# Hybrid Mamba-2 and attention trunk on eight cores: second half's z projection brought forward, one conv tap moved off VectorE, halo taps batched, a new instruction order

## The chip, the cores and the metric

The kernel runs on the 8 cores of one Trainium2 chip. Each core takes one of the 8 sequences of the batch whole, so the cores run the same program on different data and exchange nothing. The time is the device time of the slowest core in microseconds (us). The median of the runs of one kernel is what is compared.

## What is computed

The trunk has two layers over 2048 tokens of width 1024. What matters here is the first layer's mixer and the two feed-forward blocks:

```python
def mamba2_mixer(h, in_proj, conv_w, conv_b, dt_bias, A_log, D, gnorm, out_proj):
    zxbcdt = h @ in_proj
    z, xBC, dt = jnp.split(zxbcdt, [SSM_INNER, SSM_INNER + SSM_CONV_DIM], axis=-1)
    xBC = jax.nn.silu(causal_dwconv(xBC, conv_w, conv_b))          # width 4
    ...
    y = ssd_chunked(xs, dt, A, Bm, Cm) + xs * D[:, None]           # scan over chunks
    y = group_rms_norm(y * jax.nn.silu(z), gnorm, SSM_GROUPS)      # 8 groups
    return y @ out_proj

def conv_ffn(x, norm_g, w_in, conv_w, conv_b, w_down):
    gate, val = jnp.split(rms_norm(x, norm_g) @ w_in, [FFN_DIM], axis=-1)
    gate = causal_dwconv(gate, conv_w, conv_b)                     # width 3
    return (jax.nn.silu(gate) * val) @ w_down
```

x gains mixer(norm(x)), then conv_ffn; the second layer gains a sliding-window attention with rotary positions and a second conv_ffn. z of a token needs only the normed input of that token; the conv of a token needs the three tokens before it; the scan carries a state from chunk to chunk.

## The kernel before

**Work and stages.** The 2048 tokens are cut into two halves of 1024. The mixer's 8 channel groups g times 2 halves h give 16 units, in the order of `units` (all groups of half 0, then all of half 1). The program is laid out in five stages, marked at the end of `build`: A0 (units 0 to 7, with the projection of unit 8), A1+F00 (units 8 to 15 beside the output projection and the feed-forward of half 0), F01+T0 (output projection and feed-forward of half 1 beside the attention of half 0), F10+T1 (second feed-forward of half 0 beside the attention of half 1), F11 (second feed-forward of half 1, alone).

**A unit** has two parts. `P_gen(i)` projects: four conv kinds (two of x, then B, then C), each 16 matmuls of 128x512 into a pair of PSUM banks; ScalarE takes the pair out with bias and the last tap's weight into `acc` (L264), VectorE adds the other three taps from PSUM with a `scalar_tensor_tensor` each (`stt`, L279), ScalarE applies SiLU. Then z: 64 matmuls of 128x256 in two tiles, and SiLU into `zB`. The last three columns of a half 0 conv go to `halo_m`; in half 1 each of the three taps adds its halo with a small `stt` of 3, 2 or 1 columns. `S_gen(i)` does the scan: `S_head` transposes x and B by DMA on SP's queue (`xk`, `Bt`, L325) and scales on GpSimd (`xdd`), `S_exp` builds the decays for the next unit (`E`), `S_core` runs the chunks (the state `prevF`, its copies `prevB` on GpSimd, the product with z into `yg` on GpSimd, the group norm `grs`, the scaled `yn` on VectorE), `S_tail` transposes `yn` by DMA into `yT`, which the output projection reads. In half 0 `P_gen` uses two PSUM pairs in turn, in half 1 one, since the feed-forward uses the other banks.

**Weights** are loaded by DMAs that GpSimd issues (`wload`, L318): a ring `wa` of 3 buffers for the mixer and the attention, a ring `wf` of 4 for the rest, 512 KB each. Inputs, spills and transposes go through SP's queue. Rotary tables are computed by `rope_tables` at unit 4 (some 30 VectorE instructions of 128x512 and two Sin) and written to DRAM, from where the attention reads them.

**Order.** Nothing is ordered by hand within a stage: `inter` interleaves generators by their planned TensorE time into one list, and `schedule` then simulates the engines with assumed costs. An engine that is free takes, of the instructions that are ready in the simulation, the one with the smallest `prio`. What comes out is a fixed order on each engine's queue, with semaphore waits: on the chip an instruction that has to wait holds all that is behind it on its engine. `prio` is the place in the list, plus a `boost`:

```python
        op.prio = op.idx + self.boost
...
    PE_A, PE_O, PE_F, PE_T = 248.0, 55.0, 228.0, 125.0
    SKEW = 0.9
...
    run(inter((A_gen(8, 16), PE_A * SKEW), (chain(outp_gen(0), ffn_gen(0, 0)), PE_O + PE_F)))
```

## Time and profile before

| | us |
|---|---|
| median of 3 runs | 2021.59 |
| lowest and highest | 2018.05, 2031.34 |
| the profiled execution's own time | 2026.74 |
| span of its slowest core, from first to last instruction | 2025.7 |
| spans of the other cores | 2000.9 to 2018.9 |

| engine | busy, us | share of the span |
|---|---|---|
| TensorE | 1851.9 | 91% |
| VectorE | 1337.8 | 66% |
| ScalarE | 1091.4 | 54% |
| GpSimd | 720.3 | 36% |

A row of the profile names the line of the kernel (mostly that of a helper, so the tile's name says more), the engine (PE is TensorE, DVE is VectorE, ACT is ScalarE, POOL is GpSimd, SPq is SP's queue), output and inputs with shapes, then busy time and the mean duration of one in ns, then the time for which the engine sat idle just before them and what ended that. Busy time of matmuls is somewhat longer than their part in the pipeline, because their ends are modelled. PEclk is the granted TensorE clock as a share of 2.4 GHz.

### The profile page before, as it was taken

Reading aid. Unit: us, or ns where it says so; the run is one execution under the profiler, and the core shown is the slowest. Engines: PE = TensorE matmul, PEld = TensorE weight load, DVE = VectorE, ACT = ScalarE, POOL = GpSimd, SP = SyncE. Lnnn points to the kernel's source line nnn. Section 1 sums busy time; section 2 is a strip of 40 time slices with the busy share of each in tenths; the row PEclk is TensorE's granted clock in tenths of the full one; section 3 lists DMA queues with packets and bytes.
Section 4 is the critical chain, followed back from the end, with each engine's and each line's share of the span. In section 5 each row is a group of like instructions: output and inputs, shape, how many; then the busy total and the mean of one; then the engine's idle time right before and its main releaser. Section 6 shows DMA issues by size and latency. Waiting matters only on the chain.

```text
span 2025.7 us, 30699 instructions; the slowest of 8 cores (2000.9 to 2025.7 us)
## 1 busy us (share of the span) xinstructions
PE 1851.9 (91%) x9980; PEld 903.9 (45%) x9980; DVE 1337.8 (66%) x2134; ACT 1091.4 (54%) x1521; POOL 720.3 (36%) x921
## 2 busy tenths in 40 slices
PE   5898767779999999999798999999899999999999
PEld 2454434434555455545343344334433443444444
DVE  5787886656777777777656646666666566655522
ACT  5676667656655555563546527554675457523310
POOL 2355445423533233335624312533436126310000
PEclk9788889889999999999998999999899999999999
DMA  8645355726555554657653355344342653275544
GB/s 202 128 83 93 67 111 96 132 43 103 103 92 91 91 91 88 107 85 162 176 99 58 53 94 91 69 75 81 70 81 48 104 88 63 47 156 77 79 68 130
DMA packets 153996, 191.12 MB, mean 94 GB/s; under 512 B 106480, under 2 KB 114160, under 8 KB 153840
## 3 DMA queue, kind: packets, MB, share of 16 engines
q0 software_dynamic: 34704, 123.81, 36.6%
q1 hardware_dynamic: 119136, 65.34, 13.9%
q8 instruction: 84, 1.38, 0.3%
q14 instruction: 72, 0.59, 0.1%
HBM read 274.62 MB, written 15.20 MB: 143 GB/s over the span
## 4 chain that ended last, share of the span: by engine, by line
PE 79%; DVE 7%; issue 6%; DMA 3%; ACT 3%; POOL 2%; SPq 0%; DVEq 0%; POOLq 0%; ACTq 0%
PE ps L239 78%; PE ps L244 1%; DVE acc_122 L279 1%; DVE acc_121 L279 1%; DMA xs_149<-x 1%; DMA xk_130<-xc_126 1%; DVE facc_176 L279 0%; DMA xk_129<-xc_126 0%; DVE uF L268 0%; DVE facc_177 L279 0%; DMA xk_130<-xc_125 0%; DMA yT_77<-yn_81 0%; DMA wf_58<-wout 0%; POOL grs L268 0%; DVE t_86 L268 0%
## 5 line engine op out<-in xcount | busy, mean ns | idle before, releaser
L264 ACT ACT_TABLE_LOAD x176 | 225.8, 1283 | 100.5 <-PE ps L239 27.8
L279 DVE SCALAR_TENSOR_TENSOR facc_176<-ps,cst,facc_176 128x1023 f32<-128x1023 f32 x88 | 112.6, 1279 | 59.0 <-ACT facc_176 L264 58.3
L279 DVE SCALAR_TENSOR_TENSOR acc_121<-ps,cst,acc_121 128x1023 f32<-128x1023 f32 (+2 forms) x96 | 122.5, 1276 | 30.6 <-ACT acc_121 L264 30.2
L279 DVE SCALAR_TENSOR_TENSOR facc_177<-ps,cst,facc_177 128x1023 f32<-128x1023 f32 x88 | 112.5, 1278 | 39.8 <-ACT facc_177 L264 39.1
L279 DVE SCALAR_TENSOR_TENSOR acc_122<-ps,cst,acc_122 128x1023 f32<-128x1023 f32 (+2 forms) x96 | 122.5, 1276 | 13.5 <-ACT acc_122 L264 12.6
L239 PE MATMUL ps<-hF,wf_57 128*128 128x512 bf16 x544 | 129.2, 382 | 1.6 <-DVE halo_f L295 0.8
L239 PE MATMUL ps<-hF,wf_56 128*128 128x512 bf16 x544 | 128.1, 383 | 0.7 <-DVE facc_177 L279 0.5
L239 PE MATMUL ps<-hF,wf_58 128*128 128x512 bf16 x512 | 122.7, 383 | 3.6 <-DVE facc_177 L279 2.5
L239 PE MATMUL ps<-hF,wf_59 128*128 128x512 bf16 x512 | 120.7, 379 | 3.2 <-DVE uF L268 1.3
L239 PE MATMUL ps<-hT_108,wa_54 128*128 128x512 bf16 x256 | 77.4, 443 | 19.7 <-DVE acc_121 L279 12.3
L264 ACT ACTIVATE facc_176<-ps,cst 128x1024 f32<-128x1024 f32 x44 | 52.9, 1202 | 63.6 <-PE ps L239 63.6
L239 PE MATMUL ps<-wa_55,hT_108 128*128 128x256 bf16 x512 | 74.9, 299 | 8.1 <-DVE acc_122 L279 4.5
L239 PEld LDWEIGHTS ps<-hF,wf_57 128*128 128x128 bf16 x544 | 52.7, 98 | 64.1 <-issue 6.4
L239 PEld LDWEIGHTS ps<-hF,wf_56 128*128 128x128 bf16 x544 | 52.8, 99 | 63.7 <-issue 5.9
L264 ACT ACTIVATE facc_177<-ps,cst 128x1024 f32<-128x1024 f32 x44 | 52.8, 1200 | 50.4 <-PE ps L239 50.3
L239 PEld LDWEIGHTS ps<-hF,wf_58 128*128 128x128 bf16 x512 | 49.4, 98 | 64.7 <-issue 10.8
L239 PEld LDWEIGHTS ps<-hF,wf_59 128*128 128x128 bf16 x512 | 48.7, 98 | 61.7 <-issue 7.9
L239 PE MATMUL ps<-hT_109,wa_54 128*128 128x512 bf16 x256 | 65.9, 406 | 10.5 <-DVE acc_121 L279 8.3
L264 ACT ACTIVATE sg_178<-facc_176 128x1024 bf16<-128x1024 f32 x44 | 46.5, 1056 | 52.9 <-DVE facc_176 L279 52.7
L264 ACT ACTIVATE sg_179<-facc_177 128x1024 bf16<-128x1024 f32 x44 | 46.4, 1055 | 49.7 <-DVE facc_177 L279 49.5
L239 PE MATMUL ps<-wf_57,uF 128*128 128x512 bf16 x264 | 71.4, 383 | 1.6 <-DVE uF L268 1.6
L239 PE MATMUL ps<-wf_56,uF 128*128 128x512 bf16 x264 | 72.3, 383 | 0.2 <-DVE x_68 L268 0.2
(560 smaller groups left out, 4531.8 us busy)
## 6 DMA issues: line engine op xcount, KB each, us to landing
wf_56<-wfin POOLq DMA_DIRECT2D x22, 512.0 KB, 6.1
wf_57<-wfin POOLq DMA_DIRECT2D x22, 512.0 KB, 6.0
wf_58<-wfin POOLq DMA_DIRECT2D x22, 512.0 KB, 6.0
wf_59<-wfin POOLq DMA_DIRECT2D x22, 512.0 KB, 6.0
wa_53<-wA POOLq DMA_DIRECT2D x16, 512.0 KB, 6.4
wa_54<-wA POOLq DMA_DIRECT2D x16, 512.0 KB, 6.5
wa_55<-wA POOLq DMA_DIRECT2D x16, 512.0 KB, 7.0
wf_56<-wfdn POOLq DMA_DIRECT2D x9, 512.0 KB, 4.9
```

Source lines behind the costliest of these rows:

```text
L239: return self.add("pe", lambda e: e.matmul(out, lhsT, rhs, start=start, stop=stop, **kw), [lhsT, rhs] + ([] if start else [out]), [out], c)
L244: return self.add("pe", lambda e: e.transpose(out, in_, ident), [in_, ident], [out], c)
L264: return self.add("act", lambda e: e.activation(out, in_, func, **kw), rd, wr, c, table=table)
L279: return self.add("dve", lambda e: e.scalar_tensor_tensor(out, in0, scalar, in1, op0, op1), rd, [out], self._c_dve(out, [in0, in1], "stt", ...
```

## The change

1. **z early.** For groups 3 to 7 (`GZ = 3`) `P_gen` of half 0 also projects z of half 1 with the same weights, applies SiLU into `zs` and writes it to DRAM (`scr_z`); `P_gen` of half 1 loads it through SP's queue and has no z matmuls for these groups. The order of the kinds within a unit changes: B and C first, z tiles between the x tiles.
2. **One tap off VectorE.** In half 0 the oldest tap (`cw0`) is made by ScalarE as a scaled copy out of PSUM (`raw`) and added by GpSimd; VectorE keeps two taps.
3. **Halos batched.** The raw halo columns are kept (`hraw`, `hrawF`), one batch on GpSimd multiplies and sums them for all channels, and half 1 adds one small `tensor_tensor` per conv instead of three `stt` (one instead of two in the feed-forward).
4. **Order.** `prio` becomes half the place in the list minus 2.75 times the longest path to the end (`cp_mix`), in the assumed costs; DMAs on GpSimd's queue count as ready 3 us later (`swdge_slack`).
5. **Moved.** The rotary tables come first in the program, with a boost of 3000 and buffers of their own; the input norm of half 1 goes tile by tile through two buffers; the scaling to `yn` moves from the end of `S_core` to `S_tail`; the bias row `bvb` and the gain row are loaded later.

```diff
+        if self.cp_mix:
+            rank = {}
+            for op in reversed(ops):
+                r = 0.0
+                for u in op.users:
+                    if rank[u] > r:
+                        r = rank[u]
+                c = min(op.cost.values())
+                if op.dma is not None:
+                    c += 2.0 + op.dma / 290e3
+                elif not (op.engs == ("pe",)):
+                    c += 0.1
+                rank[op] = r + c
+            for op in ops:
+                op.prio = (1 - self.cp_mix) * op.prio - self.cp_mix * 5.5 * rank[op]
...
+                        if u.dma is not None and u.engs == ("pool",):
+                            u.ready += self.swdge_slack
...
+    swdge_slack = 3.0
+    cp_mix = 0.5
...
     def normA1(t4):
+        rv = rs[:, 3, :]
         for i in range(4):
...
+            xv, xn = xs1[i % 2][:], xnA1[i % 2][:]
...
+            K.act(xn, xv, AF.Square, scale=1.0 / 32.0, accum=ssq[:, 3, i:i + 1])
+            K.ts(rv[:, i:i + 1], ssq[:, 3, i:i + 1], EPS, None, OP.add, eng="pool")
+            K.tt(rv[:, i:i + 1], rv[:, i:i + 1], nhalf[:, 0:1], OP.pow, eng="pool")
+            K.stt(xn, xv, rv[:, i:i + 1], growA[:], OP.mult, OP.mult)
...
+    P_ORDER = [2, 3, 4, 0, 1, 5]
+    P_ORDZ = [2, 3, 6, 4, 0, 1, 7, 5]
+    GZ = 3
...
+    TAP_ACT = (0, 1, 2, 3)
...
+    def halo_taps():
+
+        K.tt(halo_m[:], hraw[:], C("cw0").unsqueeze(2).to_broadcast([128, 32, 3]), OP.mult, eng="pool")
+        for s in (2, 1):
+            tmp = htmp[:, :, 0:s]
+            K.tt(tmp, hraw[:, :, 3 - s:3], C(f"cw{3 - s}").unsqueeze(2).to_broadcast([128, 32, s]), OP.mult, eng="pool")
+            K.tt(halo_m[:, :, 0:s], halo_m[:, :, 0:s], tmp, OP.add, eng="pool")
...
+        order = P_ORDER
+        if g >= GZ:
+            order = P_ORDZ if h == 0 else [2, 3, 0, 1]
+            if h == 1:
+                K.dma("sp", zB[u][:], scr_z[g].ap(), f"zl{u}")
...
+                K.act(zd.rearrange("p a n -> p (a n)"), pp, AF.Silu)
+                if kind >= 6:
+                    K.dma("sp", scr_z[g].ap()[:, t4 * 4:(t4 + 1) * 4, :], zd, f"zs{zc[0] % 4}")
...
-            for s in (1, 2, 3):
-                K.stt(acc[:, s:1024], pp[:, 0:1024 - s], C(f"cw{3 - s}", j), acc[:, s:1024], OP.mult, OP.add)
-                if h == 1:
-                    K.stt(acc[:, 0:s], halo_m[:, g, kind, 3 - s:3], C(f"cw{3 - s}", j), acc[:, 0:s], OP.mult, OP.add)
-            if h == 0:
-                K.copy(halo_m[:, g, kind, 0:3], pp[:, 1021:1024])
+            if h == 0 and kind in TAP_ACT:
+                raw = rawB[tc[0] % 2]
+                tc[0] += 1
+                K.act(raw[:, 0:1021], pp[:, 0:1021], AF.Copy, scale=C("cw0", j))
+                for s in (1, 2):
+                    K.stt(acc[:, s:1024], pp[:, 0:1024 - s], C(f"cw{3 - s}", j), acc[:, s:1024], OP.mult, OP.add)
+                K.copy(hraw[:, j, :], pp[:, 1021:1024])
+                K.tt(acc[:, 3:1024], acc[:, 3:1024], raw[:, 0:1021], OP.add, eng="pool")
+            else:
+                for s in (1, 2, 3):
+                    K.stt(acc[:, s:1024], pp[:, 0:1024 - s], C(f"cw{3 - s}", j), acc[:, s:1024], OP.mult, OP.add)
...
+                    K.tt(acc[:, 0:3], acc[:, 0:3], halo_m[:, j, :], OP.add)
...
     def S_tail(i, q):
         g, h = units[i]
+        for c in range(4):
+            K.ts(ynB[q][:, :, c, :], ygB[c // 2][:, c % 2, :].rearrange("p (a n) -> p a n", a=2), grs[:, q, c:c + 1], None, OP.mult)
...
-            if i == 4:
-                rope_tables()
-            gens = [(S_gen(i), 10.4)]
+            if i == 7:
+                halo_taps()
+            gens = [(boosted(S_gen(i), SB), 10.4)]
...
-                gens.insert(0, (P_gen(i + 1), 20.8))
+                gens.insert(0, (P_gen(i + 1), 27.8 if 3 <= i + 1 < 8 else (13.8 if i + 1 > 10 else 20.8)))
...
+            K.tt(acc[:, 0:2], acc[:, 0:2], halo_f[:, j, :], OP.add)
...
-    PE_A, PE_O, PE_F, PE_T = 248.0, 55.0, 228.0, 125.0
+    PE_A, PE_O, PE_F, PE_T = 213.0, 55.0, 228.0, 125.0
...
+    K.boost = 3000
+    rope_tables()
+    K.boost = 0
     normA0()
```

`SB` is 0, so `boosted` changes nothing. Each feed-forward of half 0 gets three small GpSimd instructions after its last gate that make `halo_f` from `hrawF`.

## Rows read from the trace of the kernel before

**Rows 1.** Windows by stage, slowest core: length, PE, PEld, DVE, ACT, POOL, PEclk, DMA, GB/s.
```profile
0.00:30.00 30.00, 8.39 (x66) 6.46 (x67) 13.72 (x39) 13.64 (x24) 10.19 (x25) 1.00 0.90 213
30.00:386.00 356.00, 290.91 (x1826) 162.12 (x1825) 281.65 (x463) 244.44 (x359) 164.54 (x222) 0.85 0.54 101
386.00:985.00 599.00, 558.10 (x3414) 294.78 (x3412) 433.13 (x788) 334.24 (x484) 229.85 (x320) 0.98 0.56 101
556.00:985.00 429.00, 412.33 (x2522) 218.39 (x2520) 324.52 (x574) 234.57 (x334) 163.27 (x227) 1.00 0.56 102
985.00:1420.00 435.00, 402.83 (x1902) 177.48 (x1902) 270.58 (x386) 225.69 (x312) 158.93 (x173) 0.97 0.46 87
1420.00:1790.00 370.00, 359.69 (x1660) 156.47 (x1661) 233.21 (x325) 218.14 (x292) 140.06 (x150) 0.98 0.42 73
1790.00:2026.00 236.00, 231.93 (x1119) 106.59 (x1116) 105.51 (x138) 55.25 (x53) 16.73 (x32) 1.00 0.53 101
```

**Rows 2.** The chain that ended last, 30 to 386 us by line, and its longest piece.
```profile
by line: PE ps L239 54.4%; issue 11.6%; DMA xk_130<-xc_126 4.3%; DVE acc_122 L279 3.6%; DMA xk_129<-xc_126 2.4%; DVE acc_121 L279 2.2%; DMA xk_130<-xc_125 2.1%; POOL grs L268 1.2%; DVE yn_80 L274 1.1%; ACT L264 1.1%; POOL xdd_132 L268 1.1%;
...
1796.73 225.34 PE ps L239 x1043
```

**Rows 3.** Groups of instructions on PE: z of half 1, z and C of half 0.
```profile
L239 PE MATMUL ps<-wa_55,hT_109 128*128 128x256 bf16 x512 | 60.6, 272 | 0.3 <-DVE acc_122 L279 0.3
L239 PE MATMUL ps<-wa_55,hT_108 128*128 128x256 bf16 x512 | 74.9, 299 | 8.1 <-DVE acc_122 L279 4.5 <-DVE acc_121 L279 3.1 <-DVE halo_m L295 0.4
L239 PE MATMUL ps<-hT_108,wa_54 128*128 128x512 bf16 x256 | 77.4, 443 | 19.7 <-DVE acc_121 L279 12.3 <-DVE halo_m L295 6.9 <-DVE acc_122 L279 0.5
```

**Rows 4.** Windows of the slowest core in which the rotary tables are made.
```profile
205.00:250.00 45.00, 34.09 (x224) 19.32 (x223) 39.90 (x68) 28.36 (x38) 19.63 (x25) 0.85 0.34 64
250.00:294.00 44.00, 27.14 (x157) 14.24 (x155) 36.10 (x63) 28.90 (x44) 17.94 (x22) 0.84 0.57 123
```

**Rows 5.** Rotary tables by tile: number, ns min/median/max, first and last start.
```profile
L295 DVE CAST rt_posf<-rt_posi x1: 415/415/415, 233.6 to 233.6; 128x512 f32<-128x512 int32 x1
L264 ACT ACTIVATE rt_tb_215<-rt_ang x1: 630/630/630, 280.2 to 280.2; 128x512 f32<-128x512 f32 x1
```

**Rows 6.** Groups of instructions on ACT, 30 to 386 us.
```profile
L264 ACT ACT_TABLE_LOAD x55 | 70.6, 1283 | 20.6 <-DVE acc_121 L279 10.5 <-DVE rt_ang L275 3.7 <-DVE acc_122 L279 3.2
L264 ACT ACTIVATE acc_121<-ps,cst 128x1024 f32<-128x1024 f32 x16 | 19.2, 1198 | 22.7 <-PE ps L239 22.6
L264 ACT ACTIVATE z_123<-ps 128x1024 bf16<-128x1024 f32 x8 | 8.1, 1019 | 2.0 <-PE ps L239 1.9
```

**Rows 7.** Groups on DVE: a conv's taps (30 to 386 us), halo taps (whole span).
```profile
L279 DVE SCALAR_TENSOR_TENSOR acc_121<-ps,cst,acc_121 128x1023 f32<-128x1023 f32 (+2 forms) x48 | 61.1, 1274 | 18.8 <-ACT acc_121 L264 18.6
L279 DVE SCALAR_TENSOR_TENSOR acc_121<-halo_m,cst,acc_121 128x1 f32<-128x1 f32 (+2 forms) x48 | 15.0, 313 | 0.0
L279 DVE SCALAR_TENSOR_TENSOR facc_176<-halo_f,cst,facc_176 128x1 f32<-128x1 f32 (+1 forms) x44 | 15.3, 347 | 0.0
```

**Rows 8.** A group on POOL, 386 to 960 us, of the added tap's size.
```profile
L268 POOL TENSOR_TENSOR x_60<-x_60,bob 128x1024 f32<-128x1024 f32 x1 | 2.4, 2359 | 1.1 <-DVE xnB_184 L274 1.1
```

**Rows 9.** Like instructions of unlike duration, DVE and POOL, 30 to 386 us.
```profile
L268 DVE TENSOR_TENSOR RT_120<-AR_116,hmb 128x512 bf16<-128x512 bf16 x4 | 5.6, 1396 | 0.3 <-PE ps L239 0.3
L268 DVE TENSOR_TENSOR RT_120<-AR_115,hmb 128x512 bf16<-128x512 bf16 x4 | 1.7, 426 | 0.0
L295 POOL CAST prevB_94<-prevF_90 128x256 bf16<-128x256 f32 x6 | 6.8, 1136 | 14.7 <-DVE prevF_90 L268 14.7
L295 POOL CAST prevB_95<-prevF_90 128x256 bf16<-128x256 f32 x6 | 2.4, 406 | 4.2 <-DVE prevF_90 L268 4.2
```

**Rows 10.** Waits, 0 to 405 us: total, times, longest.
```profile
POOL wa_53 L318 <- PE ps L239: 23.3, 6, 14.6
...
DVE yn_81 L274 <- POOL grs L268: 18.4, 5, 6.4
```

**Rows 11.** SP's issues of the state's spill: number, ns min/median/max, first and last start.
```profile
L318 SPq DMA_DIRECT2D scrst<-prevF_89 x4: 343/444/899, 111.6 to 386.1; - x4
```

More of the change, by code:

```diff
@@ L472, in emit @@
             src = {}
-            for d in op.deps:
+            for d in sorted(op.deps, key=lambda o: o.idx):
                 if d.eng == e == "pe" and d.dma is None:
@@ L485, in emit @@
                 kn = dict(kn)
-                for k in sorted(need, key=lambda k: -src[k].start):
+                for k in sorted(need, key=lambda k: (-src[k].start, k)):
                     if kn.get(k, 0) >= need[k]:
@@ L699, in build @@
     scr_st = [K.scratch(f"scrst{g}", [128, 256], F32) for g in range(8)]
+    scr_z = [K.scratch(f"scrz{g}", [128, 8, 256], BF16) for g in range(8)]
     scr_y = [[K.scratch(f"scry{q}_{k}", [128, 4, 512], BF16) for k in range(4)] for q in range(2)]
@@ L824, in norm @@
                     K.evac(dst(2 * k2 + k), pb[:, k, :], scale=C(gname, 2 * k2 + k))
-    def norm_x(tiles, xn, junk, grow, dst, sem):
-        rv = norm_stats(tiles, junk)
-        for i in range(4):
-            xv = xn[xnc[0] % len(xn)]
-            xnc[0] += 1
-            K.stt(xv[:], tiles[i], rv[i], grow, OP.mult, OP.mult)
-            K.dmat(dst(i), xv[:], f"{sem}{i}")
     yT = [K.sb(f"yT{q}", [128, 16, 512], BF16, Y0 + 16384 * q) for q in range(2)]
@@ L982, in rope_tables @@
         posi, posf, ang, kf = [bufs[n][:] for n in names[:4]]
-        for q in range(4):
-            K.dma("sp", posi[32 * q:32 * q + 32, :], pos_d[0:1, q * 512:(q + 1) * 512].partition_broadcast(32), f"pos{q}")
-        K.copy(posf, posi)
+        K.copy(posf, posv[:])
         TWO_PI = 2.0 * math.pi
@@ L1016, in P_gen @@
         u = i % 2
-        for kind in range(4):
-            if kind % 2 == 0:
-                w = wload("wA", (3 * g + kind // 2) * 2048, 2048, (8, 256), "A")
+        ws = {}
+        order = P_ORDER
[3 more added lines that the diff above has]
+                K.dma("sp", zB[u][:], scr_z[g].ap(), f"zl{u}")
+        for kind in order:
+            t = min(kind // 2, 2)
+            if t not in ws:
+                ws[t] = wload("wA", (3 * g + t) * 2048, 2048, (8, 256), "A")
+            w = ws[t]
             tl = PB[h][pt[0] % len(PB[h])]
             pt[0] += 1
+            pp = pair(tl)
+            if kind >= 4:
+                t4 = kind % 2
+                hh = 1 if kind >= 6 else h
+                for k in range(4):
+                    tok = (t4 * 4 + k) * 128
+                    for kc in range(8):
+                        K.mm(ps[:, 2 * tl + k // 2, (k % 2) * 256:(k % 2 + 1) * 256], hT[hh][:, kc, tok:tok + 128], w[:, kc, :],
+                             start=(kc == 0 and k % 2 == 0), stop=(kc == 7), skip=True)
+                if kind < 6:
+                    zd = zB[u][:, t4 * 4:(t4 + 1) * 4, :]
+                else:
+                    zd = zs[zc[0] % 4][:]
+                    zc[0] += 1
+                K.act(zd.rearrange("p a n -> p (a n)"), pp, AF.Silu)
+                if kind >= 6:
+                    K.dma("sp", scr_z[g].ap()[:, t4 * 4:(t4 + 1) * 4, :], zd, f"zs{zc[0] % 4}")
+                yield 3.5
+                continue
             for n2 in range(2):
@@ L1194, in S_gen, with boosted @@
                 S_tail(*tails.pop(0))
+    SB = 0
+    def boosted(g, v):
+        while True:
+            K.boost = v
+            w = next(g, None)
+            K.boost = 0
+            if w is None:
+                return
+            yield w
     def A_gen(i0, i1):
@@ L1520, in build @@
     K.mark("A0")
+    K.boost = 3000
+    rope_tables()
+    K.boost = 0
     normA0()
```

72 lines of the change are left out of this document (38 added, 34 removed).

## The prediction

> **What bounds the kernel now.** I read first the windows by stage, cut where the program's stages hand over, then the chain of waits within the first stage, then the groups by line and the waits there.
>
> In the windows the reader is to see two kinds of stage [rows 1]. From 556 to 985 us TensorE is busy for 412.3 of 429 us at full clock (PEclk 1.00): that stretch is the scan of half 1 beside the feed-forward of half 0, and a TensorE instruction less there is time less. The last stage (231.9 of 236), the one before it (359.7 of 370) and the one from 985 to 1420 (402.8 of 435) are of the same kind. The first stage, 30 to 386 us, is not: TensorE is busy for 290.9 of 356 us, VectorE for 281.7, ScalarE for 244.4, GpSimd for 164.5, and none of them is full. The granted clock is 0.85 there, so part of TensorE's own busy time is half-speed work between its pauses. The chain in that stretch is TensorE for 54% only, 12% issue, the rest a mixture of DMA transposes, the conv's VectorE steps and GpSimd [rows 2]. So A0 is bound by its hand-overs, with TensorE idle for 65 us, and the later stages by TensorE.
>
> **The change part by part.** The sum is made against the profiled execution's own 2026.74 us (span 2025.7); the median of the runs is 5.1 us lower, and I take the forecast down by as much at the end.
>
> *z out of the saturated stretch.* Five of eight groups lose their 64 z matmuls in half 1: 320 instructions. The whole group of 512 is 60.6 us of busy time [rows 3], so 320 are 37.9 us. From the last stage's longest piece, 1043 matmuls in 225.34 us [rows 2], one of 512 columns takes 0.216 us from start to start, one of 256 therefore 0.108, and 320 of them 34.6 us. I take 36, between the two. It lies in the stretch where TensorE is 96% busy, so I count all of it: -36 (-33 to -38). Five loads of z weights on GpSimd's queue and ten SiLU of about 1.02 us on ScalarE go with it, at nothing, since neither engine is near full there.
>
> *z into A0.* The same 320 matmuls come into the first stage, at 36 us. What hides them is TensorE's idle time. The two groups that read `wa_54` and `wa_55` in half 0 waited 19.7 and 8.1 us, nearly all on VectorE's conv steps, which hold the PSUM pair [rows 3]: 27.8 us that z tiles, put between conv tiles and needing no VectorE, can fill. The other 8 us find room in the remaining 37 us of idle time, most of it short. If TensorE is kept going, its clock should also rise from 0.85, which gives something back. Taken: 0. If this cover is absent, +36; below nothing I set no more than the clock, -10.
>
> *One tap from VectorE to ScalarE and GpSimd.* 32 convs of half 0. VectorE loses 32 x 1.274 = 40.8 us [rows 7]. ScalarE gains 32 copies with a scale; the nearest row is the first step of the same conv at 1.198 us [rows 6], so 38.3 us, and with ten SiLU of z at 1.019 us, 10.2 more: 48.5. GpSimd gains 32 additions of 1021 columns; the nearest row is an addition of 1024 float columns at 2.36 us [rows 8], so 75.5 us. In the 356 us VectorE then has 241 us, ScalarE 293 (82%), GpSimd 240 (67%). The conv's PSUM pair comes free one VectorE step earlier, but the SiLU after it comes about 1.1 us later (2.36 against 1.27). Behind the copy on ScalarE stand the next conv's first step and the table loads, 55 of them for 70.6 us [rows 6]. Cost of ScalarE's fuller queue between 0 and all of its 48.5; I take +6, nearer to the lower end, because 112 us of ScalarE's 356 are idle.
>
> GpSimd's share has a second price. Equal instructions take unequal times there: `RT` 426 ns with one buffer and 1396 with the other, `prevB` 406 and 1136 ns [rows 9]. The conv's `stt`, which read one operand from PSUM, stay at 1274. So some pairs of VectorE and GpSimd instructions hold each other up. Each half 0 unit issues 22 VectorE instructions with SBUF operands (8 `E`, 2 `RT`, 8 `yn`, 4 `Dd`), 176 in all. GpSimd's busy share rises by 21 points (164.5 to 240 of 356); a catch costs at mean half a tap, 1.2 us: 176 x 0.21 x 1.2 = 44 us of VectorE's time at most, which would eat the 41 us that it loses. VectorE is not the fullest engine then, so I take +4, between 0 and +20.
> The Trainium skill (SBUF — State Buffer, section "Who interferes with whom") speaks against this part: a VectorE instruction with two SBUF inputs and a GpSimd instruction that reads SBUF exclude each other for the whole of the one that came first. `RT`'s rows agree with it, and so does the unmoved `stt`; by the rule all 32 taps are such partners, and the 44 us of the bound would be the sum's, not 4.
>
> *Rotary tables.* They run on VectorE from 233.6 to 280.2 us [rows 5]. In the two windows around them TensorE is busy for 61.2 of 89 us (69%) [rows 4], in the other 267 us of the stretch for 229.7 (86%): 15 us of TensorE's time is lost there. In the first 30 us VectorE is busy for 13.7 [rows 1], so 16 us of the tables' work fits while the inputs arrive. Gain between 0 and 15; taken -12. The position loads are small and stand in the same queue as the inputs; if they came ahead of them, they would cost about 0.44 us each [rows 11], four of them under 2 us: in the bounds.
>
> *yn later.* VectorE waits for `grs` ahead of `yn`, in one group alone 18.4 us in five waits [rows 10], with the next conv's steps behind it. Moved behind the next head in the list, the wait gets shorter: 0 to -15; taken -4, as VectorE is not full any more.
>
> *Halos.* In half 1 of the mixer 96 small instructions of 0.31 us become 32, in the feed-forwards 88 of 0.35 become 44 [rows 7]; some 20 and 15 us of VectorE's time. VectorE is 72% busy there and TensorE sets the pace, so only the steps on the chain count: -2 (0 to -8). The batches on GpSimd are a handful of small instructions: 0.
>
> *z through DRAM.* SP's queue gets ten stores in A0 and five loads in half 1, at about 0.44 us each [rows 11]: 4.4 us of A0's queue, in which the transposes for `xk` and `yT` stand, and these are on the chain. A store that waits for its SiLU holds them. 0 to +6; taken 0, as the order puts it where its data are there. The norm of half 1 through two buffers has more than 40 us to spare: 0.
>
> *The new order.* It touches every queue, and no row of before prices it. TensorE's idle time from 985 to 1790 is 32 + 10 us [rows 1]: a better order can win some 20 of it, a worse one lose as much or more. Taken 0 (-20 to +30).
>
> Sum: -36 + 0 + 6 + 4 - 12 - 4 - 2 + 0 + 0 = -44; 2026.7 - 44 = 1982.7, and 5.1 lower 1977.6: **1978 us**. Of the 44 us, 38 come after 386 us and 6 before.
>
> **The rivals.** *A: A0 shrinks too.* VectorE has 79% of the stage now and loses 41 + 20 us; PSUM pairs come free earlier. Then A0 is limited by TensorE, 291 + 36 - 10 for the clock = 317 us, at the 93% that the next stage reaches (558.1 of 599 [rows 1]): 341, 15 less than 356, of which the forecast has 6 already, and an order that wins 20 later. 1978 - 9 - 20 = 1949. For it: VectorE is the engine that TensorE waits for in A0. Against: ScalarE at 293 of 341 would be 86% full with a table load every few instructions.
>
> *B: ScalarE takes VectorE's place.* First step, copy and SiLU of a conv stand in one queue; if all 48.5 us are on the path instead of 6, the time is 1978 + 42 = 2020, no change. For it: chain steps wait for ScalarE already; against: its idle share.
>
> *C: GpSimd's queue, slower than before.* A tap waits in GpSimd's queue behind whatever is there: a weight load that waits for TensorE (6 waits, 23.3 us, the longest 14.6 [rows 10]), the scan's state copies and products. And these, which are on the scan's chain, wait behind a tap of 2.36 us. Each conv then costs 1.1 us for the slower addition and about 2 us of waiting; 32 x 3.1 = 99 us, half of it hidden by the second `acc` buffer: +50. With 20 for the held-up VectorE instead of 4 it is 1978 + 50 + 16 = 2044. It decides from the point at which A0 grows by more than the 36 us that half 1 loses.
> By the skill's rule above at its full 44 us, on top of the forecast, the time would be 1978 + 40 = 2018; by itself it does not reach the slower side.
>
> *D: the order undoes it.* If the scan of half 1 and the feed-forward no longer end together, what is left over of the scan runs alone, at A0's pace of 356 / 8 = 44.5 us a unit, of which TensorE works 290.9 x 0.85 / 8 = 31 at full clock: 13.5 us lost per unit; two units, 27. 1978 + 27 = 2005. For it: one list order decides the balance; against: the planned 213 us of `PE_A` is 35 below the old 248, which is the z removed.
>
> **How the numbers follow.** Forecast 0.50, A 0.17, B 0.13, C 0.10, D 0.10. About 1% (20 us) is what a measurement of this kernel tells from no change, so faster means below 2001. The forecast's own range, 1960 to 2000, is faster; A too; B and D are within 1% (D's near half, 0.02, faster); C is slower, and 0.02 of the worse ends of B and D. Faster 0.69, same 0.19, slower 0.12. The range goes from 1940 (A and a little of its far end) to 2030 (all of B and D, not C).
>
> **What would show it.** Right: from the end of A0 to the attention's start the stage is some 36 us shorter with TensorE still at about 96%; in A0 TensorE's busy share rises to about 0.9 and its clock above 0.85, `acc` groups on VectorE have 64 long taps instead of 96, the new GpSimd group is near 2.36 us and the waits of TensorE for VectorE fall below 28 us; A0 keeps its length within 15 us. Wrong: A0 longer by 20 us or more with long waits of ScalarE's SiLU for GpSimd (C) or of VectorE for ScalarE (B); a stretch of half 1 after the feed-forward with TensorE below 0.8 (D). A time above 2001 would mean that z's matmuls were not hidden or that the order cost what they saved.

## The result and the profile after

The changed kernel takes 1990.4 us (median of 4 runs, 1987.8 to 1993.1) against 2020.7 of the kernel before on the same chip: a ratio of 0.984, with an interval of 0.981 to 0.988. It is faster by 30 us; the forecast was 1978. In some executions, whatever the kernel, half of the cores or all get a lower clock and take longer: the times and ratios below leave these out. The spans of its eight cores went from 2000.9–2025.7 to 1974.5–1986.2 us.

The windows by stage of its slowest core, cut at its own hand-overs; the columns are those of [rows 1]:

```profile
30.00:386.00 356.00, 294.15 (x2086) 179.92 (x2084) 277.44 (x429) 270.01 (x380) 224.55 (x257) 0.94 0.56 104
544.70:940.20 395.50, 375.88 (x2179) 184.35 (x2178) 316.67 (x533) 236.26 (x333) 165.95 (x230) 0.99 0.59 108
945.00:1385.00 440.00, 408.71 (x1947) 179.53 (x1946) 263.14 (x364) 244.81 (x331) 157.33 (x172) 0.98 0.47 89
1385.00:1750.00 365.00, 353.53 (x1634) 151.70 (x1633) 228.92 (x313) 223.53 (x297) 141.28 (x153) 1.00 0.43 72
1750.00:1986.00 236.00, 231.91 (x1121) 106.68 (x1118) 101.26 (x116) 55.37 (x53) 16.82 (x32) 1.00 0.50 104
```

The second line is the stretch that lost z: it answers to the fourth of [rows 1], is 33.5 us shorter, and TensorE is still busy for 95% of it. The last stage is what it was. The first line is the surprise. VectorE gave up a tap of every conv, 40.8 us, and yet its busy time went only from 281.65 to 277.44; TensorE's share of the stage is 0.83, not 0.9. What did rise is its granted clock, from 0.85 to 0.94 on the slowest cores (0.91 to 0.95 at the mean of the eight): in the same 356 us TensorE ran 260 matmuls more, in only 3 us more of busy time.

The groups of 30 to 386 us show who filled VectorE again (busy time, mean of one in ns, idle time before and what ended it, as in [rows 7] and [rows 9]):

```profile
L239 PE MATMUL ps<-wa_56,hT_110 128*128 128x256 bf16 x490 | 69.6, 288 | 5.9 <-DVE acc_123 L280 4.8 <-DVE acc_124 L280 0.7 <-DVE hraw L295 0.4
L280 DVE SCALAR_TENSOR_TENSOR acc_123<-ps,cst,acc_123 128x1023 f32<-128x1023 f32 (+1 forms) x32 | 40.9, 1277 | 13.5 <-ACT raw_144 L264 13.2
...
L268 POOL TENSOR_TENSOR acc_123<-acc_123,raw_144 128x1021 f32<-128x1021 f32 x16 | 34.1, 2134 | 28.6 <-DVE acc_123 L280 28.6
L268 POOL TENSOR_TENSOR acc_124<-acc_124,raw_145 128x1021 f32<-128x1021 f32 x16 | 32.1, 2006 | 19.8 <-DVE acc_124 L280 19.8
L264 ACT ACTIVATE raw_145<-ps,cst 128x1021 f32<-128x1021 f32 x16 | 17.8, 1114 | 0.0
...
L268 DVE TENSOR_TENSOR E_104<-E_104,CB_108 128x512 bf16<-128x512 bf16 x7 | 11.2, 1599 | 0.8 <-ACT E_104 L264 0.8
L274 DVE TENSOR_SCALAR yn_83<-yg_89,grs 128x256 bf16<-128x256 bf16 x12 | 9.3, 806 | 1.7 <-POOL grs L268 1.7
...
L268 DVE TENSOR_TENSOR E_100<-E_100,CB_107 128x512 bf16<-128x512 bf16 x7 | 7.8, 1108 | 0.0
...
L268 DVE TENSOR_TENSOR E_103<-E_103,CB_108 128x512 bf16<-128x512 bf16 x7 | 3.0, 435 | 0.0
```

The added operations are close to what was taken for them: the copy 1.11 us (taken 1.198), the addition on GpSimd 2.07 at mean (2.36), and the tap with PSUM as an input has kept its time (1277 ns, before 1274). What changed is the product `E`, the same instruction on the same shape: 435 ns in one buffer, 1108 in the next, 1599 in a third. In the profile of before its eight buffers took 409 to 686 ns; the longest and the shortest:

```profile
L268 DVE TENSOR_TENSOR E_98<-E_98,CB_105 128x512 bf16<-128x512 bf16 x7 | 4.8, 686 | 1.0 <-ACT E_98 L264 1.0
...
L268 DVE TENSOR_TENSOR E_101<-E_101,CB_106 128x512 bf16<-128x512 bf16 x7 | 2.9, 409 | 0.0
```

Over the 56 of them in 30 to 386 us, the mean went from 471 to 861 ns; that of the 52 `yn` from 396 to 629. Sorted by what GpSimd was at when the instruction began, over the eight cores of the changed kernel: 165 `E` that began beside an idle GpSimd took 413 ns at mean, 97 that began during an addition of the tap 1727; `yn` 278 (189) and 1950 (37).

What TensorE waits for follows. The waits of the first stage (total us, times, longest):

```profile
PE ps L239 <- DVE acc_123 L280: 13.3, 11, 2.8
...
PE ps L239 <- DVE E_100 L268: 5.9, 4, 1.7
PE ps L239 <- DVE E_99 L268: 5.5, 4, 2.6
...
PE ps L239 <- DVE E_104 L268: 4.3, 4, 1.4
POOL wa_57 L318 <- PE ps L239: 3.8, 2, 2.5
```

Summed over all rows of this view, TensorE waits 40.5 us for VectorE, against 35.0 before. The conv's part of it fell (`acc` and halo copies 27.7 to 14.4 us), but that for `E` rose from 3.5 to 18.9. Its waits for ScalarE fell from 26.7 to 12.1 us. And the waits of GpSimd's weight loads for TensorE are down to the 3.8 us of the last line. In the profile of before they were 59 us in all; beside the buffer of [rows 10]:

```profile
POOL wa_54 L318 <- PE ps L239: 13.2, 6, 3.9
POOL wa_55 L318 <- PE ps L244: 11.0, 1, 11.0
POOL wa_54 L318 <- PE ps L244: 10.1, 1, 10.1
```

The chain in the same stretch says it in shares; beside the conv's steps, `E` and the scaled copy `raw` are on it now, and the transposes for `xk` have shrunk from the 8.8% of [rows 2]:

```profile
by line: PE ps L239 44.8%; issue 13.9%; DMA xq_154<-x 3.2%; DVE acc_123 L280 3.2%; DVE acc_124 L280 2.9%; DVE E_104 L268 2.3%; DMA wa_56<-wA 2.1%; DMA xk_132<-xc_127 1.7%; SPq L325 1.7%; DVE yn_82 L274 1.7%; ACT raw_144 L264 1.4%; DVE E_100
```

### The profile page after: what moved, and what is told of

It is laid out like the page before. It is cut to its first block, busy times and chain, and to the rows that moved or that the text cites. A ratio compares the mean times of both kernels' runs of the same rounds, so it can differ in the third digit from the quotient of the medians.

```text
span 1986.2 us, 30588 instructions; the slowest of 8 cores (1974.5 to 1986.2 us)
## 1 busy us (share of the span) xinstructions
PE 1819.1 (92%) x9980; PEld 889.0 (45%) x9980; DVE 1309.5 (66%) x1994; ACT 1148.2 (58%) x1575; POOL 785.1 (40%) x967
## 4 chain that ended last, share of the span: by engine, by line
PE 76%; DVE 9%; issue 6%; DMA 4%; ACT 3%; POOL 2%; SPq 1%; DVEq 0%; ACTq 0%; POOLq 0%
PE ps L239 75%; DVE uF L268 1%; PE ps L244 1%; DMA yT_79<-yn_83 1%; DVE acc_123 L280 1%; DMA cm<-cm 1%; DMA wf_61<-wfin 1%; DVE acc_124 L280 1%; DMA xq_154<-x 1%; DVE E_104 L268 0%; DVE yn_83 L274 0%; DMA wa_56<-wA 0%; SPq L325 0%; DVE yn_82 L274 0%; DMA xk_132<-xc_127 0%
## 5 line engine op out<-in xcount | busy, mean ns | idle before, releaser
L264 ACT ACT_TABLE_LOAD x198 | 254.0, 1283 | 105.9 <-PE ps L239 25.7
L239 PE MATMUL ps<-hF,wf_59 128*128 128x512 bf16 x544 | 143.8, 379 | 5.0 <-DVE uF L268 3.6
L239 PE MATMUL ps<-hF,wf_58 128*128 128x512 bf16 x544 | 140.2, 379 | 3.9 <-DVE uF L268 3.5
L239 PE MATMUL ps<-hF,wf_61 128*128 128x512 bf16 x512 | 131.5, 379 | 7.1 <-DVE uF L268 7.0
L239 PE MATMUL ps<-hF,wf_60 128*128 128x512 bf16 x512 | 131.8, 379 | 4.4 <-DVE uF L268 4.3
L280 DVE SCALAR_TENSOR_TENSOR acc_123<-ps,cst,acc_123 128x1023 f32<-128x1023 f32 (+2 forms) x80 | 102.1, 1277 | 20.6 <-ACT raw_144 L264 13.2
L280 DVE SCALAR_TENSOR_TENSOR acc_124<-ps,cst,acc_124 128x1023 f32<-128x1023 f32 (+2 forms) x80 | 102.0, 1275 | 11.2 <-ACT acc_124 L264 10.6
L239 PE MATMUL ps<-wa_56,hT_111 128*128 128x256 bf16 x512 | 72.8, 292 | 16.1 <-DVE acc_123 L280 8.4
L239 PE MATMUL ps<-wf_58,uF 128*128 128x512 bf16 x264 | 81.7, 379 | 1.6 <-DVE x_62 L268 1.5
L239 PE MATMUL ps<-wf_60,uF 128*128 128x512 bf16 x264 | 81.6, 379 | 1.7 <-DVE uF L268 1.5
L239 PE MATMUL ps<-wf_61,uF 128*128 128x512 bf16 x264 | 81.3, 379 | 0.0
L239 PE MATMUL ps<-wf_59,uF 128*128 128x512 bf16 x264 | 80.6, 379 | 0.0
L239 PE MATMUL ps<-wa_56,hT_110 128*128 128x256 bf16 x512 | 72.6, 288 | 5.9 <-DVE acc_123 L280 4.8
L264 ACT ACTIVATE sg_184<-facc_182 128x1024 bf16<-128x1024 f32 x44 | 46.4, 1055 | 46.6 <-DVE facc_182 L268 38.8
```

Source lines behind the costliest of these rows:

```text
L239: return self.add("pe", lambda e: e.matmul(out, lhsT, rhs, start=start, stop=stop, **kw), [lhsT, rhs] + ([] if start else [out]), [out], c)
L264: return self.add("act", lambda e: e.activation(out, in_, func, **kw), rd, wr, c, table=table)
L280: return self.add(eng, lambda e: e.scalar_tensor_tensor(out, in0, scalar, in1, op0, op1), rd, [out], c)
```

## The experiments

All times below come with the ratio to the kernel before, measured on the same chip in the same batch. The three stretches are means over the eight cores of the profiled execution: "first" runs from the start to the first gate matmul of the feed-forward, "scan 2" from there to the last transpose of the scan's result (`yst`), "later" from there to the last gate matmul. What comes after that is 266 to 268 us in every kernel.

| kernel | us | ratio (95%) | first | scan 2 | later |
|---|---|---|---|---|---|
| before | 2020.7 | | 542.8 | 432.9 | 770.3 |
| after | 1990.4 | 0.984 (0.981–0.988) | 539.4 | 395.6 | 779.0 |
| e1_no_z | 2012.2 | 0.996 (0.992–1.000) | 542.1 | 414.9 | 778.2 |
| e2_dve_taps | 1983.6 | 0.981 (0.978–0.985) | 531.8 | 395.9 | 779.1 |
| e3_old_order | 2020.8 | 1.001 (0.999–1.004) | 566.5 | 403.4 | 771.1 |
| e4_write_only | 1998.3 | 0.989 (0.986–0.992) | 543.8 | 396.7 | 779.3 |
| e5_order_alone | 2005.1 | 0.993 (0.991–0.995) | 530.3 | 415.9 | 781.1 |
| e6_path_first_half | 1985.8 | 0.984 (0.982–0.985) | 541.2 | 396.5 | 773.5 |
| e7_dve_taps_path_first | 1977.5 | 0.979 (0.977–0.981) | 532.3 | 396.5 | 774.1 |
| e8_fill_same_order | 1973.1 | 0.977 (0.975–0.980) | 520.5 | 395.7 | 778.9 |
| e9_tables_late | 1969.1 | 0.974 (0.969–0.978) | 524.2 | 396.5 | 774.0 |
| e10_yn_early | 1985.5 | 0.981 (0.976–0.986) | 536.6 | 395.7 | 774.8 |
| e11_no_slack | 2012.9 | 0.995 (0.989–1.001) | 558.0 | 397.4 | 780.4 |
| e12_dve_taps_old_order | 1996.9 | 0.988 (0.982–0.995) | 545.5 | 408.2 | 770.7 |

e1 to e4 ran in one batch (before: 2021.1), e5 to e8 in a second (2019.0), e9 to e12 in a third (2024.4); across batches the ratios are compared, and a difference of 0.001 is 2 us. Except for e5, which starts from the kernel before, and e9 and e10, which start from e7, each edit is against the changed kernel. The order is worked out anew from the instructions, so an edit also moves instructions that it does not name; where it did not, the text says so.

What TensorE does in the first stretch, again as means over the eight cores (granted clock as a share of 2.4 GHz):

| kernel | matmuls | TensorE busy, us | idle, us | clock |
|---|---|---|---|---|
| before | 2770 | 429.2 | 113.5 | 0.92 |
| after | 3091 | 445.5 | 93.9 | 0.96 |
| e1_no_z | 2836 | 432.7 | 109.4 | 0.94 |
| e3_old_order | 3100 | 459.1 | 107.4 | 0.93 |
| e4_write_only | 3091 | 452.9 | 90.9 | 0.94 |
| e8_fill_same_order | 3091 | 439.8 | 80.8 | 0.96 |
| e11_no_slack | 3092 | 458.9 | 99.1 | 0.93 |

Nearly the same matmuls keep TensorE busy for 440 us at a mean clock of 0.96 in one order and for 459 at 0.93 in another: of what e3 and e11 lose against the changed kernel, and e4 against e8, half or more is TensorE's own busy time.

**e1_no_z: z back in half 1.**

```diff
-    GZ = 3
+    GZ = 8
-                gens.insert(0, (P_gen(i + 1), 27.8 if 3 <= i + 1 < 8 else (13.8 if i + 1 > 10 else 20.8)))
+                gens.insert(0, (P_gen(i + 1), 20.8))
-    PE_A, PE_O, PE_F, PE_T = 213.0, 55.0, 228.0, 125.0
+    PE_A, PE_O, PE_F, PE_T = 248.0, 55.0, 228.0, 125.0
```

> The changed kernel (1990 us) with z of the second half left where it was (all eight groups late, planned times as before). Theory (the gain is z: 36 us leave the saturated stretch and the first stage takes them up in its idle time): 1990 + 36 less the little that the first stage gets shorter, 2015 to 2026; the stretch from the first gate of the feed-forward to the last transposes of the scan about 430 us again, that gate's start moved by less than 12 us. Rival (z only changes places, the gain is the taps, tables and order): the first gate starts 25 us or more earlier and the time stays at 1990 to 2002.

Without the early z the gain falls from 30 to some 8 us: z is worth some 22, less than the theory's 25 to 36. The first stage does not get shorter when z leaves it (542.1 against 539.4), so z in it is hidden: with z TensorE is idle for 15.5 us less there and busy for 12.8 us more, for 255 matmuls more. The second scan is 19 us longer without early z, not 36. Its window in this kernel, from the first gate matmul on, to be held against the second line of the windows above:

```profile
544.90:962.10 417.20, 397.89 (x2423) 209.18 (x2421) 310.95 (x515) 230.61 (x324) 163.70 (x227) 0.99 0.61 106
```

TensorE's busy time differs by 22 us, and 244 matmuls, though 306 z matmuls are gone (338 to 32 in these two windows). With z in the first stage, more of the other work is left for the second: the convs' matmuls there went from 320 to 337, the scan's (with a few of the norms) from 677 to 706, the output projection's from 32 to 48. In e1 that work was done before the first gate matmul.

**e2_dve_taps: all taps on VectorE again.**

```diff
-    TAP_ACT = (0, 1, 2, 3)
+    TAP_ACT = ()
```

> The changed kernel with all four conv taps of half 0 on VectorE again. Theory (what VectorE sheds it gives back in the products E, which rose from 0.47 to 0.86 us beside GpSimd's taps, so the move is worth little): E back to about 0.47 us, the first gate of the feed-forward within 8 us of its start in the changed kernel, time 1984 to 2000. Rival (without that relief the first stage can't take z up): VectorE 280 to 320 us busy from 30 to 386, first gate 20 to 40 us later, time 2010 to 2030.

Some 6 us faster than the changed kernel, with overlapping intervals, and 8 us shorter in the first stage: the move of the tap has gained nothing. The products are short again; in the groups of 30 to 386 us (the trace of the experiments gives all buffers as one name):

```profile
L268 DVE TENSOR_TENSOR E<-E,CB 128x512 bf16<-128x512 bf16 x56 | 29.2, 536 | 1.2 <-ACT E L264 1.2
```

536 ns against the 861 with the tap on GpSimd, and 390 against 629 for `yn`: over the 56 and 52 of them, 31 of the 41 us that VectorE had been spared.

**e3_old_order: the list's place alone decides.** The 3 us of `swdge_slack` stay.

```diff
-    cp_mix = 0.5
+    cp_mix = 0.0
```

> The changed kernel with the old order (place in the list alone), the late DMA issue kept. Theory (the new order costs the 7 to 10 us by which the time from the end of the scan to the last gate matmul of the second feed-forward grew, and gives nothing much before): that stretch back to 768 to 773 us from 779, time 1978 to 1990. Rival (the new order carries the first stage, where z and the taps could not be placed without it): first gate 15 us or more later, time 2000 to 2020.

With everything else in place the whole gain is gone: 2020.8. The second scan keeps most of it (403.4; later 771.1), but the first stage is 27 us longer than with the new order and 24 longer than before. Its waits in 30 to 386 us:

```profile
POOL wa L318 <- PE ps L239: 13.8, 3, 10.6
...
PE ps L239 <- DMA xk<-xc: 10.1, 2, 6.7
```

TensorE waits 10 us for transposes of x, and GpSimd's loads, with the taps behind them, wait for TensorE for 13.8 us instead of 3.8. Of the 27 us, 13.6 are TensorE's busy time and 13.5 its idle time.

**e4_write_only and e8_fill_same_order: GpSimd as long, but reading nothing.** Both leave the fourth tap out of the sum and lose what `acc` held; they keep the copy on ScalarE, and GpSimd writes instead of adding.

```diff
e4:
-                K.tt(acc[:, 3:1024], acc[:, 3:1024], raw[:, 0:1021], OP.add, eng="pool")
+                K.memset(acc[:, 3:1024], 0.5, eng="pool")
+                K.memset(acc[:, 3:1024], 0.5, eng="pool")
e8:
-                K.tt(acc[:, 3:1024], acc[:, 3:1024], raw[:, 0:1021], OP.add, eng="pool")
+                av, rw = acc[:, 3:1024], raw[:, 0:1021]
+                K.add("pool", lambda e, av=av, rw=rw: (e.memset(rw, 0.5), e.memset(av, 0.5))[1], [], [av, rw], K._n(av) * 0.00225 + 0.06)
```

> The changed kernel with GpSimd's addition of the tap replaced by two fills of the same columns of acc (the fourth tap is left out of the sum and acc's content lost; all other instructions, queues and waits stay). A fill writes and reads nothing; two should take 2.0 to 2.6 us together. Theory (the long E, yn and RT come from VectorE and GpSimd both reading a second operand in SBUF): E back to 0.45 to 0.55 us at the same GpSimd load, VectorE's busy time from 30 to 386 us 20 to 35 us lower, TensorE's waits for E gone, time 1975 to 1988. Rival (GpSimd's queue or the mere load is what delays): E still above 0.75 us and the time within 5 us of the changed kernel.

e4 was to settle the contention and did not. `E` fell to 28.6 us for 56, but the time was some 8 us longer than the changed kernel's: the extra instruction had changed the list, and at 1201 of 9980 places in TensorE's queue another weight load stood. So e8 does both fills in one step of the list, with the assumed cost of the addition; the order on TensorE, VectorE, ScalarE and SP's queue is then that of the changed kernel.

> The changed kernel with each addition of GpSimd's tap replaced by two fills, one of raw and one of acc, of the same columns, in exactly the changed kernel's order on TensorE, VectorE, ScalarE and SP (the fourth tap is left out, acc's content lost). Theory after the earlier fills (VectorE's lost time is real, but VectorE is not what the first stage waits for): E at 0.45 to 0.55 us, VectorE's busy time from 30 to 386 us 25 us or more lower, first gate 0 to 6 us earlier, time 1985 to 1992. Rival (the earlier fills came out no faster only because the order changed with them): first gate 10 to 20 us earlier, time 1970 to 1981.

17 us faster (14 by the ratios), all of it in the first stage (520.5 against 539.4), as the rival had it. Its window and groups of 30 to 386 us:

```profile
30.00:386.00 356.00, 311.81 (x2244) 191.30 (x2241) 267.71 (x465) 284.88 (x406) 229.20 (x311) 0.96 0.63 116
```

```profile
L268 DVE TENSOR_TENSOR E<-E,CB 128x512 bf16<-128x512 bf16 x60 | 36.9, 634 | 1.0 <-ACT CB L264 0.6 <-ACT E L264 0.4
L274 DVE TENSOR_SCALAR yn<-yg,grs 128x256 bf16<-128x256 bf16 x56 | 26.2, 646 | 9.8 <-POOL grs L268 9.8
...
L1098 POOL MEMSET acc<- 128x1021 f32 x32 | 31.2, 974 | 0.0
L1098 POOL MEMSET raw<- 128x1021 f32 x32 | 30.7, 960 | 44.6 <-DVE acc L280 44.6
```

A pair of fills takes 1.93 us against the addition's 2.07, so GpSimd is held nearly as long, at the same places; some 4 us at most are that difference. `E` falls from 861 to 634 ns, 158 more matmuls get into the window, and VectorE is busy for 10 us less while it does 36 instructions more. Sorted as above, 157 `E` of the eight cores began during a fill and took 414 ns at mean, the longest 426, no more than beside an idle GpSimd (414); what is left of the lengthening stands beside GpSimd's other work, as in the kernel before. `yn` is another matter: it stays long (646 ns, after 629), and 106 that began during a fill took 1095 at mean. TensorE's waits for `E`:

```profile
PE ps L239 <- DVE E L268: 8.1, 11, 1.6
```

They were 18.9 us in the changed kernel, and all its waits for VectorE fall from 40.5 to 22.7. So most of the addition's price on GpSimd, some 14 to 17 us, is what its reading does to `E`, and not its place in GpSimd's queue. e4, whose `E` is as short, is 23 to 25 us slower than e8, 23 of it in the first stage: by so much can the order alone move this stage.

**e5_order_alone: the order on the kernel before, without any other part.** The `cp_mix` and `swdge_slack` blocks of the change, as shown there, put into the kernel before.

> The kernel before with the new order alone (path length and late DMA issue); no early z, no moved tap, nothing else. Theory (the order pays in the first stage mainly because it lets z tiles there be filler, so without z it has less to do): first gate of the feed-forward within 8 us of 543 (mean of the cores), the scan's stretch after it 10 to 18 us shorter, the later stretch 8 us longer, time 2005 to 2018. Rival (the order is worth its 31 us whatever stands in the stages): time 1985 to 1998.

It gains 15 us by itself: 12 in the first stage and, in the second half, 17 in the scan less 11 in the stretch after it. So of the 37 us by which the changed kernel's second scan is shorter than before, the order's share is 17 when it comes alone, and z's 19 when it comes last (e1); nearly the 36 us forecast for z alone, from two causes. The split depends on what else is there: taken out of the changed kernel, path length is worth only 8 us of this stretch (e3, 403.4 against 395.6).

**e6_path_first_half: path length only up to the attention.**

```diff
-            for op in ops:
+            for op in ops[:[m for m in self.marks if m[0] == "F01+T0"][0][1]]:
```

> The changed kernel with path length in the priority only up to the start of the attention's stage, place in the list after it. Theory (the new order costs 8 us in the two stages with attention): the time from the scan's last transposes to the last gate matmul of the second feed-forward 771 us instead of 779, all before unchanged, time 1979 to 1985. Rival (the longer stretch comes from what the first half leaves late): that stretch stays at 777 to 781, time 1987 to 1993.

The stretch after the scan wins back 5.5 of the 8.7 us that it had lost; the time, 2 us lower by the ratio, is within the scatter of the changed kernel's. Where TensorE is full, the new order cost a little. One trace of it are ScalarE's table loads of 985 to 1700 us, first of before, then of the changed kernel:

```profile
L264 ACT ACT_TABLE_LOAD x55 | 70.6, 1283 | 29.7 <-DVE facc_176 L279 12.8 <-DVE halo_f L295 10.4 <-PE ps L239 4.1
```

```profile
L264 ACT ACT_TABLE_LOAD x73 | 93.7, 1283 | 36.2 <-DVE facc_182 L280 12.6 <-DVE facc_182 L268 7.9 <-DVE facc_181 L268 6.4
```

18 more in this window; between the two ends of the stretch itself the count is 61 before, 75 in the changed kernel and 63 in e6, so steps that share a table stand less often together in the new order. TensorE's idle time in the stretch goes the same way, 42.2, 48.4 and 42.3 us at the mean of the cores. Whether ScalarE's 14 loads more, 18 us, are what makes TensorE wait was not tried.

**e7_dve_taps_path_first: e2's and e6's edits together.**

> The same, and all four taps of half 0 on VectorE. Theory (both gains add, they lie in different stages): first gate about 532 us, later stretch 771, time 1971 to 1980. Rival (one takes the other's place): 1981 to 1988.

1977.5, a ratio of 0.979: the two add up as far as the intervals tell. The next two start from it.

**e9_tables_late: e7 with the rotary tables at unit 4 again.** The four position loads move into the function too, and its buffers to space that is free then.

```diff
+            if i == 4:
+                rope_tables()
...
-    K.boost = 3000
-    rope_tables()
-    K.boost = 0
```

> The kernel of the run before last (all taps on VectorE, path length in the order up to the attention's stage; 1979 us, first gate at 532 as mean of the cores) with the rotary tables back at unit 4. Theory of the forecast (the tables cost the first stage about 12 us where VectorE is busy): first gate 8 to 15 us later, time 1986 to 1994. Rival (an order by path length puts them into VectorE's gaps wherever they stand in the list): first gate within 4 us, time 1976 to 1983.

This kernel is faster, against both expectations: 0.974 against 0.979, intervals that just touch, and 8 us of it in the first stage. The edit changes the tables' place in the list, their boost (which puts them behind whatever else is ready) and their loads at once, and with them the order of the rest; together the change's arrangement costs about 10 us here. The first step of the tables begins at 28.2 us in the changed kernel (the position loads are issued at 6.6 to 8.3 us, behind inputs, and land 14 us later) and the second Sin at 75.6; the first 30 us hide none of it. In e7 they run from 29 to 107 us. In e9 half of them still come early, the rest from 221 to 255 us. The windows of 30 to 180 us, of e7 and then of e9:

```profile
30.00:180.00 150.00, 116.80 (x771) 67.05 (x769) 123.41 (x194) 108.11 (x146) 65.07 (x92) 0.93 0.61 117
```

```profile
30.00:180.00 150.00, 125.20 (x843) 72.69 (x841) 128.13 (x198) 111.19 (x157) 69.71 (x104) 0.92 0.64 113
```

72 more matmuls get done there with half of the tables out of the way. VectorE is 82% busy in this stretch of e7, so the tables had moved from one crowded stretch to another.

**e10_yn_early: e7 with `yn` at the end of `S_core` again.** The two lines of `yn` in `S_tail` move back.

> The same kernel (1979 us, tables early) with the scaling to yn back at the end of S_core. Theory of the forecast (VectorE stands behind it while GpSimd makes grs): first gate 3 to 8 us later, time 1982 to 1987. Rival (the place in the list decides little here): within 2 us, 1977 to 1981.

0.981 against 0.979, 4 us, all in the first stage, as the theory had it; but one interval holds the other whole, and the order differs. An effect of `yn`'s place is not shown.

**e11_no_slack: DMAs on GpSimd's queue count as ready at once.**

```diff
-    swdge_slack = 3.0
+    swdge_slack = 0.0
```

> The changed kernel (1990 us) without the 3 us by which weight loads on GpSimd's queue count as ready later; path length stays. Theory (path length makes the order's gain): first gate within 4 us of 539, time 1986 to 1995. Rival (the late loads make it: in the first stage GpSimd's waits for TensorE are 9 us against 61 before): those waits back above 40 us, first gate 8 us or more later, time 1998 to 2010.

22 us of the 30 are gone, 19 of them in the first stage. A wait that was gone is back:

```profile
POOL wa L318 <- PE ps L239: 45.5, 11, 18.7
```

45.5 us in eleven waits, after 3.8 in two: weight loads that the order puts too early wait on GpSimd's queue for TensorE to give up their buffer, and GpSimd's taps, `grs` and state copies stand behind them. That this wait is what the 22 us are is argued, not shown: TensorE's own waits for GpSimd rise by 6 us only (3.3 to 9.1), and 13 of the 19 us are its busy time at a clock of 0.93. And the slack is no part of the gain by itself: e3 has it without path length and gains nothing, e11 has path length without it and gains 8 us, and both together gain 30. With the taps on VectorE (e2) the loads wait for 25 us, and the kernel is as fast as the changed one.

**e12_dve_taps_old_order: the taps back on VectorE under the old order.** The edits of e2 and e3 together.

> The changed kernel with the old order and all taps of half 0 on VectorE: what is left is early z, the tables, halos and the late loads. Theory (z tiles are filler in the first stage only for an order by path length; in list order they stand ahead of the x tiles that the scan waits for): first gate 550 to 562 us, time 2008 to 2019. Rival (with the old order it was GpSimd's tap that could not be placed, z is hidden by either order): first gate 532 to 545, time 1983 to 1998.

With it the two suspects form a square (ratios, all with z early, tables early, `yn` late):

| | taps on VectorE | one tap on ScalarE and GpSimd |
|---|---|---|
| list's place, slack kept | 0.988 (e12) | 1.001 (e3) |
| path length | 0.981 (e2) | 0.984 (after) |

Under the old order the tap's move costs 0.013, some 26 us, 21 of it in the first stage; under the new one 0.003, 6 us. The order gains 35 us with the move, and some 14 without it (the intervals of e12 and e2 overlap). Much of what the order brings in this change is that it pays for the taps. And e12 against before (first stage 545.5 against 542.8, the rest 24 us shorter) shows z hidden without path length too, with the slack in place.

## Why the prediction was right, and where it was not

The outcome is the likeliest case, 12 us above its number and inside its own range. That the number came so near is luck in part: z gave some 14 us less than its term and the tables' term had the wrong sign, and the new order, put at 0, made up for it. Of the signs named for being right, the shorter stage of half 1, the clock above 0.85, the 64 long taps and the unchanged length of A0 appeared; a TensorE share of 0.9 and less waiting for VectorE did not (0.83, and 40.5 us where below 28 was named).

*z out of the saturated stretch, -36: mis-sized, -22 in place.* The 36 us by which the second scan is shorter were the sign that I had named, and they appeared (37.3). The sign did not tell z from the order: e1 gives z 19 of them, e5 the order 17 by itself. The count and the price per matmul were right. The step that failed is "so I count all of it": when a tenth of a full stretch is taken out, other work, done ahead of it until then, comes in its place. Under the old order z may have been worth more: the rest after the first stage is 24 us shorter in e12 than before, which holds the halos too and was not tried without z.

*z into A0, 0: right.* e1 shows the first stage no shorter without z, and e12 the same under the old order, within 3 us each time. I had taken it that TensorE's idle time hides all of it. Less idle time is 15.5 us (e1 against the changed kernel); the clock, which I had named and put at nothing, rose from 0.94 to 0.96 beside it.

*One tap, +6 and +4: near in the sum, wrong in the parts.* e2 gives +6 in place. ScalarE's share was not seen: TensorE's waits for it fell. The contention is 14 to 17 (e8) and not 4; I took a tenth of the bound because VectorE would no longer be the fullest engine, and overlooked that `E` stands between two matmuls, so that a longer `E` is a longer wait whatever VectorE's share (TensorE waited 18.9 us for it, after 3.5). What VectorE was spared then pays for the rest, some 10 us, if e2 and e8 are set against each other; their orders differ. The Trainium skill (SBUF — State Buffer, section "Who interferes with whom") agrees with the rows: `E`, with two SBUF inputs, takes 413 ns where it begins beside an idle GpSimd, 1727 during an addition, which reads SBUF, and 414 during a fill, which reads nothing, while the tap with a PSUM input stays at 1275 ns. `yn`, with one tensor input, rose too (396 to 629) and did not fall beside fills (646), which the rule as I used it does not cover. The bound of 44 us was VectorE's time; some 30 us were measured for `E`, `RT` and `yn` together.

*Rotary tables, -12: no gain, and by e9 a cost of about 10.* The step that failed is that 16 us of their work "fits while the inputs arrive": their own input lands some 14 us after its issue at 6.6 to 8.3, and their first step begins at 28.2 us. That they do not hide there is shown; how much of the 10 us is theirs is not, with a different order behind e7 and e9 and a stage that scatters.

*yn, -4: not told from nothing* (e10, 4 us in the forecast's direction, within the scatter). *Halos, -2, and the z through DRAM, 0*: not tried alone. Nothing in the waits above names either.

*The new order, 0 (-20 to +30): -31 in place, outside the range.* It is the largest term of all. The -31 are path length with the slack in place (e3); both alone, without the other parts, are -15 (e5), and the slack is worth 22 where path length is there (e11). I had put the waits on GpSimd's queue down as rival C, whose price depends on the very waits that `swdge_slack`, a line of the same change, removes, and had not carried that line into the sum. In the later stages it cost 5 to 9 us (e6), where I had none.

Of the rivals, A's smaller first stage did not come (539.4 against 542.8); with the taps on VectorE and late tables it does (524.2, e9), but not by A's mechanism: VectorE keeps its taps there, and the order alone gives 12 us (e5) of these 19. B is not seen. C's waits are seen in e11, though even there the kernel is no slower than before. D, the scan left over alone, is not seen: on the slowest core of the changed kernel the scan's last matmul ends 4 us after the feed-forward's last of half 0 (924 and 920), before it was 22 us (978 and 956).

The terms do not add up, and what they are worth depends on the order. e4 against e8 shows some 24 us between two kernels whose instructions differ little; differences of 4 to 10 us between kernels of different order (e2, e6, e9, e10) are therefore directions at most. What is left open is why the order moves the first stage by so much: no one wait explains e4's 23 us in it, of which 13 are TensorE's busy time at a clock of 0.94 instead of 0.96, and 10 its idle time.

The best kernel is e9: z early, halos batched, path length up to the attention, the slack, `yn` late, all taps on VectorE and the tables at unit 4: 1969.1 us, 0.974 (0.969 to 0.978).

## What to carry to other kernels

Work moved to an idle engine can be paid for by instructions of another engine that run at the same time (here `E` on VectorE, from 471 to 861 ns): look at what the moved instruction does to the mean duration of its neighbours, per buffer, before the busy shares are added up. A scheduler that knows nothing of blocked queues must be told: a DMA issue that waits for a free buffer should count as ready late when compute stands behind it on the same queue (22 us here, e11, under an order by path length). And when a sign fits a term (36 us here), take that term out alone before it is believed; two other causes may add up to it.

## What was not expected of the hardware

The same VectorE product of 128x512 bf16 took from 435 to 1599 ns at the mean of one buffer of one kernel, long where it began during a GpSimd instruction such as the tap's addition (413 ns beside an idle GpSimd, 1727 there), and the longer time stands inside its own duration, so that no wait shows it. GpSimd's fills of 128x1021 floats, at 0.96 to 0.97 us, did nothing to it (414 ns), but did lengthen `yn`, a product with one scalar per partition, from 278 to 1095 ns. A table load on ScalarE took 1283 ns in every profile, and their number depends on the order: 75 in the later stretch of the changed kernel, 63 with the list's order there (e6).
